# Layer 0's projections as three products of split operands in strips of 256 columns, and the index heads of five blocks weighed and added by GpSimd

## What is computed, cut to the stage that the change touches

The change lies in layer 0 (`diff_dsa_layer`). It normalizes the rows of x, multiplies them by one wide matrix `w_in` (1024 x 3784) and splits the columns. One part is ordinary attention with two maps per head (qa, ka, va). The other is attention over 256 selected keys per query (qb, kb, vb). The selection comes from an index: eight small heads qi against one key ki, each cut at zero, weighed by wi and added; the 256 largest scores of each row are kept.

## Time and profile before

| what | value |
|---|---|
| time, three runs | 2583.99, 2590.09, 2588.89 us; median 2588.89 |
| span of the profiled execution | 2587.5 us, 1.4 us under the median; the page gives its span and no separate device time |
| TensorE busy over the span | 2414.7 us (93%) |
| VectorE busy | 1766.7 us (68%) |
| ScalarE busy | 1265.7 us (49%) |
| GpSimd busy | 517.4 us (20%) |
| first stage (`layer0_project`) | from 0 to 502.9 us |
| L521, f32 matmuls of the projections | 832 records, 366.2 us |
| L525, the same for the values | 128 records, 60.4 us |
| L1652 and L1653, the rounds | 176 of each, 162.6 and 159.4 us |

### The profile page before, as it was taken

The page is one execution under the profiler, slowest core; times in us unless marked ns, Lnnn a source line. Parts: engine busy times, 40 slices in busy tenths (PEclk is TensorE's granted clock), DMA queues, the critical chain, the costliest instruction groups (busy, mean ns, idle before and its releaser), DMA issues. The chain is left out here.

```text
span 2587.5 us, 33902 instructions
## 1 busy us (share of the span) xinstructions
PE 2414.7 (93%) x12487; PEld 1684.5 (65%) x12487; DVE 1766.7 (68%) x3295; ACT 1265.7 (49%) x2065; POOL 517.4 (20%) x506
## 2 busy tenths in 40 slices
PE   7989999999999899999998989999992999999998
PEld 3334444455555698777776769875661788888886
DVE  2599999767776321766767535507666688888886
ACT  2212111145555446556565434335444777777774
POOL 0000000011110000366767710001324111222110
PEclk9999999989999899999999999998995999999999
DMA  4011752301100323222323332031104999999995
GB/s 139 1 37 37 85 62 90 101 30 50 50 26 25 129 77 74 78 76 80 97 70 122 113 132 95 3 124 41 50 33 187 378 396 386 385 383 383 391 389 189
DMA packets 155473, 361.71 MB, mean 140 GB/s; under 512 B 35512, under 2 KB 69000, under 8 KB 155312
## 3 DMA queue, kind: packets, MB, share of 16 engines
q1 hardware_dynamic: 140128, 308.15, 32.4%
q0 software_dynamic: 15184, 51.42, 9.1%
HBM read 320.71 MB, written 38.82 MB: 139 GB/s over the span
## 5 line engine op out<-in xcount | busy, mean ns | idle before, releaser
L521 PE MATMUL ps<-l_hT,l_w 128*128 128x512 f32 (+1 forms) x832 | 366.2, 599 | 2.6 <-DVE l_hT L242 2.6
L521 PEld LDWEIGHTS ps<-l_hT,l_w 128*128 128x128 f32 (+1 forms) x832 | 156.1, 190 | 205.6 <-issue 205.5
L996 ACT ACTIVATE a_pT<-ps 128x512 f32<-128x512 f32 (+3 forms) x176 | 79.6, 484 | 180.5 <-PE ps L874 179.2
L1652 DVE MAX8 l_best<-sel 128x8 f32<-128x640 f32 (+5 forms) x176 | 162.6, 924 | 4.9
L1653 DVE MATCH_REPLACE8 sel<-l_best,sel 128x640 f32<-128x640 f32 (+5 forms) x176 | 159.4, 906 | 0.0
L1008 ACT ACTIVATE a_p<-ps,a_stat 128x384 f32<-128x384 f32 (+7 forms) x192 | 128.9, 672 | 19.8 <-DVE a_stat L1087 13.7
L2403 ACT ACTIVATE l_lat<-ps,h_stat 128x384 f32<-128x384 f32 (+7 forms) x128 | 94.1, 740 | 76.1 <-DVE h_stat L2593 40.1
L3404 POOL DMA_INDIRECT out_dram<-m_q,e_token x15 | 34.0, 2269 | 447.6 <-DVE m_q L3602 447.6
L921 PE MATMUL ps<-l_wo,a_mixT 128*128 128x512 f32 x256 | 119.7, 594 | 0.9 <-DVE a_y L1787 0.9
L1983 POOL TENSOR_TENSOR ada_acc<-ada_acc,ada_w 128x384 f32<-128x384 f32 x112 | 116.6, 1041 | 8.8
L3233 DVE TENSOR_TENSOR x_w2l<-x_raw,x_w2h 128x4096 fp32r<-128x4096 f32 x23 | 101.8, 4426 | 18.5 <-ACT x_w2h L3225 18.5
(11 more groups left out here) (651 smaller groups left out, 6138.1 us busy)
## 6 DMA issues: line engine op xcount, KB each, us to landing
x_raw<-in_w_gate SPq DMA_DIRECT2D x25, 2048.0 KB, 11.1
x_raw<-in_w_down SPq DMA_DIRECT2D x24, 2048.0 KB, 9.9
x_raw<-in_w_up SPq DMA_DIRECT2D x23, 2048.0 KB, 11.4
ada_w<-in_w_ada POOLq DMA_DIRECT2D x64, 384.0 KB, 3.7
m_ufT<-in_w_up SPq DMA_DIRECT2D x9, 2048.0 KB, 11.6
m_ufT<-in_w_down SPq DMA_DIRECT2D x8, 2048.0 KB, 12.3
l_w<-in_e_w_in SPq DMA_DIRECT2D x7, 2048.0 KB, 9.0
m_ufT<-in_w_gate SPq DMA_DIRECT2D x7, 2048.0 KB, 9.9
```

Of the source, the lines that this page charges most:

```text
L521: last = nc.tensor.matmul(self.t.ps[0:m, bank, :], w[:, c, col * P:col * P + m], hT[:, c, half * 512:(half + 1) * 512], start=c == 0, stop ...
L1652: link(nc.vector.max(best[:], line))
```

```diff
+    def dve_scale(self, e, b):
...
+        self.nc.vector.scalar_tensor_tensor(self.X(b), self.X(b), self.stat[:, 2, b:b + 1], self.gains,
+                                            ALU.mult, ALU.mult).then_inc(self.scaled, 1)
...
+    def act_high(self, e, b):
+        for i in range(self.NG):
+            g, of, high, _ = self.parts(b, i)
+            e.wait_ge(self.turned, g + 1)
+            self.nc.scalar.activation(high, of, ACT.Copy).then_inc(self.highs, 1)
+
+    def dve_low(self, e, b):
...
+            self.nc.vector.tensor_tensor(low, of, high.bitcast(F32), ALU.subtract).then_inc(self.done, 1)
...
+    def load(self, e, i):
+        s, of = self.strips[i], rows(self.strips[i].loads[0][1])
+        for half in range(2):
+            if self.earlier[i] is not None:
+                e.wait_ge(self.lows, 2 * self.place[self.earlier[i]] + half + 1)
+            e.dma_start(self.raw[half][:, :, 0:s.n], of[:, half * KD // 2:(half + 1) * KD // 2, :]).then_inc(self.raw_in[half], 16)
...
+    def act_high(self, e, i):
+        n = self.place[i]
+        if self.free[i]:
+            e.wait_ge(self.made, self.free[i])
...
+            self.k.nc.scalar.activation(high, raw, ACT.Copy).then_inc(self.highs, 1)
+
+    def pool_low(self, e, i):
...
+            e.wait_ge(self.highs, 2 * n + half + 1)
+            self.k.nc.gpsimd.tensor_tensor(low, raw, high.bitcast(F32), ALU.subtract).then_inc(self.lows, 1)
...
+            products = ((wh, xh), (wh, xl), (wl, xh)) if s.kind == "T" else ((xh, wh), (xh, wl), (xl, wh))
+            for n, (lhs, rhs) in enumerate(products):
+                last = nc.tensor.matmul(out, lhs, rhs, start=c + n == 0, stop=c == KD - 1 and n == 2)
...
+    sequence = [*high(VA0), *high(KI), *norms(0), *group(VA0, 0), *norms(1), *group(VA0, 1), *high(QI0), *norms(2, 3),
+                *high(QI1), *group(KI, 0), *norms(4), *group(QI0, 0), *norms(5), *group(QI0, 1), *norms(6), *group(QI1, 0),
+                *norms(7), *group(QI1, 1), *group(WI, 0), *pair(0, 2, 4, 6),
+                *group(KI, 1), *pair(8, 10), *group(QI0, 2), *group(WI, 1), *pair(12), *group(QI0, 3), *high(VA1), *pair(14, 16),
...
+    def pool_add(self, e, n):
+
+        score, part, weight = head_ready(e, n)
+        if work[n][1] == 0:
+            nc.gpsimd.tensor_scalar(score, part, weight, None, ALU.mult).then_inc(used, 1)
+        else:
+            nc.gpsimd.tensor_scalar(part, part, weight, None, ALU.mult).then_inc(weighed, 1)
+            e.wait_ge(weighed, n - 7 - work[n][0] + SMALL)
+            nc.gpsimd.tensor_tensor(score, score, part, ALU.add).then_inc(used, 1)
...
-            for n in range(len(work)):
-                if n >= 8:
-                    top_k(work[n - 8][0], rounds(n))
-                add_head(n)
-                if n == 16:
-                    tables.dve_lambda(e)
-            top_k(SEL_BLOCKS[-1], range(ROUNDS(SEL_BLOCKS[-1])))
+            for n in range(8):
+                dve_add(e, n)
+            top_k(SMALL)
+            tables.dve_lambda(e)
+            for b in SEL_BLOCKS[1:]:
+                top_k(b)
```

More of the change, by code:

```diff
@@ L1462, in layer0_project @@
+def layer0_project(k, a, t, early, qaT, kaT, va, qbT, kb, vw, sel, bias):
     nc = k.nc
[L1463 to L1466, removed]
+    qiT, ki, relu = early.qiT, early.ki, early.relu
     W = a["e_w_in"][0]
[L1468 to L1471, removed]
@@ L1472, in layer0_project @@
[L1472 to L1489 removed]
+    col = lambda c, n: [(0, W[:, c:c + n])]
@@ new lines, in layer0_project, with head_ready, dve_add @@
+    pr = SplitStrips(k, t, norm, strips, slots, raw, {KI: early.key_raw}, [x for what, x in sequence if what == "group"])
+    def head_ready(e, n):
+        b, h = work[n]
+        e.wait_ge(cut, n + 1)
+        if n:
+            e.wait_ge(used, n)
+        if h == 0:
+            e.wait_ge(pr.put, pr.turn[WI, b // 4] + 1)
+        return sel[:, SEL_AT[b]:SEL_AT[b] + (b + 1) * P], relu[n % 2][:, 0:(b + 1) * P], vw[:, b, 64 + h:65 + h]
+    def dve_add(e, n):
+        score, part, _ = head_ready(e, n)
+        if n == 0:
+            link(nc.vector.tensor_scalar(minus[:], vw[:, SMALL, 64:72], -1.0, None, ALU.mult))
+            nc.vector.tensor_scalar(score, part, minus[:, 0:1], None, ALU.mult).then_inc(used, 1)
+        else:
+            nc.vector.scalar_tensor_tensor(score, part, minus[:, n:n + 1], score, ALU.mult, ALU.add).then_inc(used, 1)
@@ L1569, in _ @@
                     norm.pe(e, n)
-                    continue
-                if what == "group":
+                elif what == "group":
                     if pr.turn[n] < 2:
@@ L1587, in _ @@
-                for c in range(0, width, 512):
-                    c1 = min(c + 512, width)
-                    for d in range(2):
-                        half = slice(64 * d, 64 * d + 64)
-                        last = nc.tensor.matmul(t.ps[:, 2 * d + c // 512, 0:c1 - c], qiT[half, h // 2, b * P:(b + 1) * P],
-                                                ki[half, 0, c:c1], start=True, stop=True)
-                        if c1 == width:
-                            last.then_inc(logits, 1)
+                elif what == "logits" and n % 2 == 0:
+                    b, h = work[n]
+                    if n:
+                        e.wait_ge(cut, n)
+                    else:
+                        e.wait_ge(norm.done, NB * norm.NG)
+                    if b in (SMALL, NB // 2):
+                        e.wait_ge(pr.put, pr.turn[QI0 if h < 4 else QI1, 2 * (b // 4) + h // 2 % 2] + 1)
+                    width = (b + 1) * P
+                    for c in range(0, width, 512):
+                        c1 = min(c + 512, width)
+                        for d in range(2):
+                            half = slice(64 * d, 64 * d + 64)
+                            last = nc.tensor.matmul(t.ps[:, 2 * d + c // 512, 0:c1 - c], qiT[half, h // 2, b * P:(b + 1) * P],
+                                                    ki[half, 0, c:c1], start=True, stop=True)
+                            if c1 == width:
+                                last.then_inc(logits, 1)
@@ L1641, in top_k @@
-            def top_k(b, steps):
+            def top_k(b):
                 width = (b + 1) * P
```

385 lines of the change are left out of this document (270 added, 115 removed).

## The result

| | before | after |
|---|---|---|
| time, median (range) | 2586.4 us (2583.3 to 2590.1) | 2557.0 us (2552.8 to 2557.6) |
| ratio | | 0.9883, 95% interval 0.9869 to 0.9897 |
| span of the profiled execution | 2587.5 us | 2555.5 us |
| attention's first matmul | 502.94 | 469.37 |
| VectorE done in the first stage | 489.03 | 450.75 |

What follows compares the result with a forecast made beforehand. TensorE was taken to bound layer 0's first stage, VectorE 13 us behind. With VectorE then ending at 437, the stage gained 65 us, less 2 for clock: span 2524.5, median 2526 us, range 2511 to 2553.

Steps and rivals of the forecast that it cites:

- Nothing; uncovered it would hold TensorE, which has 10 us: Bias rows' writes beside QA0 and QA1 loads, before the gate: no time lost; a strip's load took 39.1 us.
- the sum: First stage: VectorE 437, TensorE 427, so its end 65 us earlier; with 2 us for the clock, change -63 us.
- TensorE's group: Projection groups with weights stationary: 24 split matmuls take 5.6 us instead of 6.87, -66 us over 52 groups.
- Value steps: Value strip's split matmuls of 256 columns: 0.120 us each, 46 us for 384, saving 9 us.
- if its waits stayed: TensorE in the first stage: 75 us less work, ending at 427 provided its waits were unchanged.
- GpSimd's tensor_scalar: Weighing of a head on GpSimd at 1024 elements: 1.1 us, between 1.04 and 2.35; a head 3.5 us.
- the signs that the prediction named for being wrong: Rounds longer than 1.25 and 2.58 us, TensorE last, first logits after 78, or GpSimd's tensor_scalar over 2.4 us at 1024.
- VectorE: End of VectorE's first-stage chain: 437, from 437.9 without adds and waits, -10 for the start, +9 for a wait.
- the wait ahead of block 3: Head of block 3's rounds: VectorE waits once for GpSimd's last two heads, 9 us.
- Rounds beside GpSimd: VectorE's MAX8 and MATCH_REPLACE8 rounds aren't slowed by GpSimd: no cost; 1 us for the scaling and first adds.
- TensorE ends it: Rival, chance 0.12: weight loads set value groups' pace, 72 us instead of 46; TensorE ends at 453, kernel 2543.
- The other side: Rival, chance 0.05: GpSimd's instructions hold up VectorE's rounds, 160 us on its chain, ending at 597; kernel 2686.

Runs made afterwards that it cites:

- the first two experiments: Changed kernel with QA1's high part behind QA0's third group: 2541.7 us; changed kernel with bias rows' writes behind QA1's low parts instead of KB's: 2536.5 us.
- the seventh kernel: Changed kernel with QA1's high part behind QA0's third group, weighing by broadcast-weight tensor_tensor, and VA1's high and low parts behind logits 14 and 15: 2530.6 us.
- experiments 3 and 4: Changed kernel without weighing heads 1 to 7 of blocks 3 to 7: 2541.0 us; changed kernel weighing by tensor_tensor with broadcast weight: 2542.1 us.
- experiment 12: Changed kernel with two 4 KB loads on SyncE's queue, one ahead of each half of QA1, beside the bias rows' writes: 2556.1 us, one run.

## Why the prediction was wrong

- **The step that failed** is "Nothing; uncovered it would hold TensorE, which has 10 us" under Transfers. It asked when the groups of QA0 and QA1 come, not when their high parts do. A high part is an instruction of ScalarE, stands ahead of KB's groups in the order, and all of ScalarE's moves wait behind it. The load took 50 us where it counted on 39; ScalarE needed it at 183.3, while QA1's own groups come from 256.5 on; and the price was 26.3 us of TensorE, whose waits the sum had left as they were. Shown by the first two experiments: by the ratios 13 to 20 us come back when the two are parted, until VectorE ends the stage. The first's 2541.7 lies inside the range forecast for the change.
- **The rest of the miss is VectorE's chain.** Without the stall attention starts at 453.9, the forecast was 438 [502.94 - 65]. The points on GpSimd and VectorE below give 13.8 of these 16 us, as read in the changed kernel.
- **TensorE's group** 5.6: 5.44. **Value steps** 0.120: 0.120 (168.64, 168.76, 168.88, ...). The prices of the products were right, and "if its waits stayed" was not. In the seventh kernel, with the stall gone and GpSimd faster, TensorE is done at 426.6, where the forecast said 427; that they meet is luck in part, as 52 groups of 5.44 and not 5.6 take 8 us off the sum, which waits have filled again.
- **GpSimd's tensor_scalar** 1.1, bounds 1.04 to 2.35: 2.85, outside the bounds. I bounded it by the number of tensors read. It is one of the signs that the prediction named for being wrong, as is TensorE ending the stage. It makes a head 5.2 us and not 3.5, and TensorE's logits wait for it. In the profiles of experiments 3 and 4, with the stall still there, TensorE is done 20 and 12 us earlier.
- **VectorE** 437: 450.8. Its first add came at 73.9 (forecast 69.9), the wait ahead of block 3 is 12.8 (9), and the masks, 3.6 us before, take 6.2 beside GpSimd. That is 10.4 of the 13.8. Most of the other 3.4 was an error of the sum: it took off the adds' busy time, 38.7 us, but in the kernel before a next instruction starts 0.08 us before an add ends. A round with an add takes 3.52 us (347.04 to 350.56) and one without 2.32, so an add of 1.28 us cost 1.20, and the 40 adds some 3 us less than their busy time:

```profile
344.72 1.09 DVE L1652 MAX8 l_best<-sel 128x8 f32<-128x896 f32 x1
...
347.04 1.09 DVE L1652 MAX8 l_best<-sel 128x8 f32<-128x896 f32 x1
...
349.36 1.28 DVE L1638 SCALAR_TENSOR_TENSOR sel<-l_relu,vw,sel 128x1024 f32<-128x1024 f32 x1
350.56 1.09 DVE L1652 MAX8 l_best<-sel 128x8 f32<-128x896 f32 x1
```

- **Rounds beside GpSimd** unaffected: right. MAX8 of 1024 is 1228 ns before and after, MATCH_REPLACE8 1208. The mask of 512 is the case against: 426 before, and

```profile
L1890 DVE MAX8 l_best<-sel 128x8 f32<-128x1024 f32 x32 | 39.3, 1228 | 1.1
...
L1892 DVE TENSOR_SCALAR sel<-sel 128x512 f32<-128x512 f32 x1 | 1.7, 1744 | 0.0
```

- **Rivals.** "TensorE ends it" came true by another way: value groups cost what was forecast. The other side didn't come. Faster, given 0.91, came true; the range was too narrow because it had no case for a load that ScalarE waits for.

So one failure was in the order of the program, a load in front of unrelated work of ScalarE, and one in a price, GpSimd's tensor_scalar. The seventh kernel mends both and has 2530.6, where the forecast for the change was 2526; VectorE, done at 444.0 and not 437, still ends its stage.

## What to carry to other kernels

When a change gives an in-order engine an instruction that needs a load, put the load's landing against the time of that instruction and name all that is queued behind it, on every engine; the consumer two steps on is the wrong place to look. Where two engines end a stage a few us apart, relieving the one that ends last is worth the gap at most, and relieving the other only what it gives the last (here 9 us, as TensorE's gaps got shorter and its clock higher): plan the two together and sum each engine's chain with its waits. A broad write of short rows needs a time in which nobody is about to wait for a load.

## What the runs showed of the hardware

- GpSimd at 1024 elements: tensor_scalar with a weight from memory 2846 ns, tensor_tensor 2390, tensor_tensor with a broadcast weight 1895; at 512 elements 1567, 1282 and 1041 (experiment 4 has the last form). A second input broadcast along the row is cheaper than a full one, and the one-tensor form is the dearest.
- Loads beside the broadcast writes get about one packet for one: of writes and loads 117 and 112 moved from 180 to 190 us, 116 and 82 from 190 to 200, 125 and 124 from 200 to 210. A half of QA1 is 512 packets of 1 KB. None moved between its issue at 166.9 and 175 us, 610 of both halves' 1024 from 175 to 215, and 446 packets of loads from 215 to 220, as the writes ended. In the kernel before, a load of 2048 KB beside these writes, 1040 packets of 2 KB, took 39.1 us. So a load is slow here whatever its size; that the number of its packets is the whole reason isn't shown, as 4 KB in 128 packets took 41 us in experiment 12. The Trainium skill, "DMA: Bandwidth & Descriptors", section "Queues, rings and completion order", says that each DMA engine goes round-robin between queues, packet by packet, and that a completion is counted only when that engine's earlier writes have landed. The packet counts agree with the first, if a packet of the profile is one of the page's; whether the second adds to the small loads' 41 us, no run here separates.
- VectorE's mask, a tensor_scalar, grew from 426 to 1744 ns at 512 and from 359 to 1316 at 384 while GpSimd added, its MAX8 not at all. The Trainium skill, "SBUF — State Buffer", section "Who interferes with whom", has tensor_scalar among the operations that can take the port pair shared with GpSimd, for which the second to start waits. The growth of the masks agrees with it. So does MAX8, which reads one tile: the section says that a VectorE instruction with at most one input in SBUF, outside the two-port modes, does not contend.
- TensorE, idle from 196 to 222 us, had a granted clock of 0.55 from 200 to 210 and 0.50 (1.2 GHz) from 210 to 230, where it had worked again from 222 on (0.92 from 230 to 240).
